# Mixer tiles of a two-layer model: one product of 512 columns for two of 256, in a ring of four PSUM banks

## The reference, cut to what matters

```python
def short_conv_mixer(h, w_in, conv_w, w_out):  # h: 256 tokens x 1024
    bg, cg, v = jnp.split(h @ w_in, 3, axis=-1)
    return (bg * causal_dwconv(cg * v, conv_w)) @ w_out

x = x + short_conv_mixer(rmsnorm(x, mix_norm[0]), a_w_in[0], a_conv[0], a_w_out[0])
x = x + conv_ffn(rmsnorm(x, ffn_norm[0]), ...)          # 2816 hidden features
...                                                      # attention layer, second conv_ffn, final norm
```

## Time and profile before

| | us |
|---|---|
| median of 3 runs | 623.72 (623.45 to 626.21) |
| the profiled execution | 623.19 |
| its span, from first to last instruction | 621.1 |
| TensorE busy | 606.9 (98%) |
| VectorE busy | 484.5 (78%) |
| ScalarE busy | 390.1 (63%) |
| mean granted TensorE clock | 0.999 |

### The profile page before, as it was taken

The page is one execution under the profiler, slowest core; times in us unless marked ns, Lnnn a source line. Parts: engine busy times, 40 slices in busy tenths (PEclk is TensorE's granted clock), DMA queues, the critical chain, the costliest instruction groups (busy, mean ns, idle before and its releaser), DMA issues.

```text
span 621.1 us, 11391 instructions
## 1 busy us (share of the span) xinstructions
PE 606.9 (98%) x3772; PEld 532.6 (86%) x3772; DVE 484.5 (78%) x954; ACT 390.1 (63%) x725; POOL 64.1 (10%) x82
## 2 busy tenths in 40 slices
PE   8999999999999999999999899999999999999995
PEld 8999998988888888888989777777988888888884
DVE  4888657788888887777877799938688888887765
ACT  7545336666666666668556488727766666666644
POOL 0110011000000000011131156610100000000010
PEclk9999999999999999999999999999999999999999
DMA  8797442465565655761476401033355555555521
GB/s 343 290 337 241 169 141 97 155 218 200 188 222 201 201 204 186 281 246 36 136 246 211 133 2 35 2 102 136 123 204 208 201 204 203 202 203 188 193 101 68
DMA packets 30352, 109.55 MB, mean 176 GB/s; under 512 B 3387, under 2 KB 3659, under 8 KB 30188
## 3 DMA queue, kind: packets, MB, share of 16 engines
q1 hardware_dynamic: 29756, 106.97, 48.9%
q0 software_dynamic: 560, 2.12, 1.0%
HBM read 108.01 MB, written 1.07 MB: 176 GB/s over the span
## 4 chain that ended last, share of the span: by engine, by line
PE 89%; DVE 5%; ACT 3%; issue 1%; DMA 1%; POOL 0%; DVEq 0%; ACTq 0%
PE bank L1244 24%; PE bank L1248 12%; PE bank L1193 10%; PE bank L1194 10%; PE bank L1195 10%; PE bank L1212 9%; PE bank L1217 4%; PE bank L1289 2%; DVE w_lo L814 1%; PE bank L1302 1%; PE bank L1571 1%; ACT work L557 1%; PE bank L1603 1%; PE bank L1596 1%; ACT w_hi L553 1%
## 5 line engine op out<-in xcount | busy, mean ns | idle before, releaser
L814 DVE TENSOR_TENSOR w_lo<-staged,w_hi 128x1024 fp32r<-128x1024 f32 x188 | 233.1, 1248 | 45.1 <-ACT w_hi L553 45.1
L553 ACT ACTIVATE w_hi<-staged 128x1024 fp32r<-128x1024 f32 x196 | 198.6, 1046 | 24.6 <-PE bank L1217 7.7
L1244 PE MATMUL bank<-gx,w_hi 128*128 128x512 f32 x640 | 159.4, 391 | 0.0
L1244 PEld LDWEIGHTS bank<-gx,w_hi 128*128 128x128 f32 x640 | 117.5, 188 | 23.0 <-DVE work L950 0.2
L1248 PEld LDWEIGHTS bank<-gx,w_lo 128*128 128x128 f32 x640 | 87.3, 190 | 6.3
L1248 PE MATMUL bank<-gx,w_lo 128*128 128x256 f32 x640 | 89.2, 282 | 0.0
L1193 PE MATMUL bank<-w_hi,y 128*128 128x512 f32 x208 | 81.5, 392 | 0.0
L1194 PE MATMUL bank<-w_lo,y 128*128 128x512 f32 x208 | 81.5, 392 | 0.0
L1195 PE MATMUL bank<-w_hi,y 128*128 128x512 f32 x208 | 80.9, 389 | 0.0
L683 ACT ACTIVATE work<-work,params 128x256 f32<-128x256 f32 x96 | 44.2, 504 | 54.3 <-DVE work L950 39.2
L697 ACT ACTIVATE y<-work 128x256 fp32r<-128x256 f32 x52 | 21.7, 418 | 77.6 <-DVE work L971 59.8
(11 more groups left out here) (182 smaller groups left out, 815.6 us busy)
## 6 DMA issues: line engine op xcount, KB each, us to landing
staged<-in_f_up SPq DMA_DIRECT2D x88, 512.0 KB, 5.1
staged<-in_f_down SPq DMA_DIRECT2D x44, 512.0 KB, 3.6
staged<-in_a_up SPq DMA_DIRECT2D x24, 512.0 KB, 6.9
staged<-in_b_up SPq DMA_DIRECT2D x24, 512.0 KB, 4.2
staged<-in_a_down SPq DMA_DIRECT2D x8, 512.0 KB, 3.6
staged<-in_b_down SPq DMA_DIRECT2D x8, 512.0 KB, 4.2
bias<-bias_rows POOLq DMA_DIRECT2D x1, 2048.0 KB, 12.1
x<-in_xt SPq DMA_DIRECT2D x1, 1024.0 KB, 9.2
```

Source lines behind the costliest of these rows:

```text
L553: nc.scalar.activation(w_hi[:, q["slot"], 0:n], staged[:, s, 0:n], ACT.Copy).then_inc(hi, 1)
L814: nc.vector.tensor_tensor(w_lo[:, q["slot"], 0:n], staged[:, s, 0:n], w_hi[:, q["slot"], 0:n].bitcast(F32), ALU.subtract).then_inc(lo, 1)
L1244: nc.tensor.matmul(dst, w_hi[:, s, kt * P:kt * P + P], gx[:, kt, :], start=kt == 0, stop=False, skip_group_check=True)
```

## The change

A mixer tile takes a whole bank. For each k-slice one product of 512 columns is made of w_hi and both parts of x, and one of 256 of w_lo and x_hi: 16 matmuls for 24. Tile (k, c) uses bank (3 (k % 2) + c) % 4, so over two units the banks go 0, 1, 2, 3, 0, 1 and start again. Before a tile whose bank was used before, TensorE waits for a count of `added`. For each tile ScalarE copies the bank's second half to the place of the result in SBUF (`parts_of`), VectorE adds the first half to it and counts `added`; the products with rstd, rstd2 and the third part follow on the sums in SBUF. The third sum stands behind the `early` remainder on VectorE, and the third copy behind the `early` lead on ScalarE. Line numbers in the changed kernel are higher: L553 becomes L563, L814 L835, L1212 and L1217 L1275 and L1279, L942 and L943 L968 and L970, L945 L976; new are L693 (the copy) and L964 (the sum).

```diff
--- before.py
+++ after.py
@@ -237,7 +237,8 @@
         squared, halved, deviated, rstd_done = sem("squared"), sem("halved"), sem("deviated"), sem("rstd_done")
         rstd_spread, rstd_ready, xn_done, xn_far, x_turned = (
             sem(n) for n in ("rstd_spread", "rstd_ready", "xn_done", "xn_far", "x_turned"))
-        lo_read = {s: sem(f"lo_read_{s}") for s in ("f0", "f1")}
+        lo_read = {s: sem(f"lo_read_{s}") for s in ("a", "f0", "f1")}
+        added = sem("added")
         padded = sem("padded")
         consts_done, table_done, rows_done, rows_copied = sem("consts_done"), sem("table_done"), sem("rows_done"), sem("rows_copied")
         rows_stored = sem("rows_stored")
@@ -317,6 +318,15 @@
         def split_of(st, t, kt):
 
             return SPLIT_AT[st] + 8 * t + kt + 1
+
+        def tile_bank(k, c):
+
+            return bank[(3 * (k % 2) + c) % 4]
+
+        def parts_of(k, c):
+
+            r = k % 2
+            return {0: shifted[:, r, 1, 2:2 + T], 1: conv[:, r, 1, :], 2: shifted[:, r, 0, 2:2 + T]}[c]
 
         def pair_of(st, k, n):
 
@@ -671,8 +681,19 @@
                 r = k % ring
                 u = k + PER[st] * i
                 early, middle, late = ahead
-                for q in early:
-                    lead(*q)
+                if st == "a":
+
+                    if k >= 2 or looped(i):
+                        act.wait_ge(y_lo_done["a"], u - 1)
+                    for c in range(3):
+                        if c == 2:
+                            for q in early:
+                                lead(*q)
+                        act.wait_ge(used_up, piece_of("a", "up", k, c)["n"] + 1 + stride("a", "up") * i)
+                        nc.scalar.activation(parts_of(k, c), tile_bank(k, c)[:, T:2 * T], ACT.Copy).then_inc(lo_read["a"], 1)
+                else:
+                    for q in early:
+                        lead(*q)
                 if st != "a":
 
                     act.wait_ge(used_up, piece_of(st, "up", k, 1)["n"] + 1 + stride(st, "up") * i)
@@ -936,14 +957,23 @@
                 u = k + PER[st] * i
                 early, middle, late = ahead
                 if st == "a":
-                    last = piece_of(st, "up", k, 2)
-
-                    dve.wait_ge(used_up, last["n"] + 1 + stride(st, "up") * i)
-                    nc.vector.tensor_tensor(shifted[:, r, 1, 2:2 + T], bank[2 * r][:, 0:T], rstd[:], ALU.mult)
-                    nc.vector.tensor_tensor(conv[:, r, 1, :], bank[2 * r][:, T:2 * T], rstd2, ALU.mult).then_inc(convolved[st], 1)
+
+                    def add(c):
+
+                        dve.wait_ge(lo_read["a"], 3 * u + c + 1)
+                        nc.vector.tensor_tensor(parts_of(k, c), tile_bank(k, c)[:, 0:T], parts_of(k, c), ALU.add).then_inc(added, 1)
+                        dve.wait_ge(added, 3 * u + c + 1)
+
+                    add(0)
+                    nc.vector.tensor_tensor(parts_of(k, 0), parts_of(k, 0), rstd[:], ALU.mult)
+                    add(1)
+                    nc.vector.tensor_tensor(parts_of(k, 1), parts_of(k, 1), rstd2, ALU.mult).then_inc(convolved[st], 1)
+                    for q in early:
+                        rest(*q)
+                    early = []
+                    add(2)
                     dve.wait_ge(convolved[st], 3 * u + 1)
-                    nc.vector.tensor_tensor(shifted[:, r, 0, 2:2 + T], bank[2 * r + 1][:, 0:T], conv[:, r, 1, :],
-                                            ALU.mult).then_inc(scaled[st], 1)
+                    nc.vector.tensor_tensor(parts_of(k, 2), parts_of(k, 2), parts_of(k, 1), ALU.mult).then_inc(scaled[st], 1)
                     halves, per, off = 1, 3, 1
                 else:
                     dve.wait_ge(lo_read[st], u + 1)
@@ -1225,13 +1255,30 @@
                 return nc.tensor.matmul(out_ap[:, 0:T], w_lo[:, s, cols], gx_hi[:, kt, :], start=False, stop=stop, skip_group_check=True)
 
             def up_a(k, i=0, cs=range(3)):
-                if k >= 2:
-
-                    pe.wait_ge(scaled["a"], k - 1 + PER["a"] * i)
+
                 for c in cs:
-                    fresh = (gx_lo_done, 0) if (k, c) == (0, 0) else (None, None)
-                    dst = bank[2 * (k % 2) + c // 2][:, c % 2 * T:(c % 2 + 1) * T]
-                    product(piece_of("a", "up", k, c), dst, gx_hi, gx_lo, c % 2 == 0, stride("a", "up") * i, *fresh)
+                    q, dst = piece_of("a", "up", k, c), tile_bank(k, c)
+                    s, move = q["slot"], stride("a", "up") * i
+                    if (k, c) != (1, 0) and k >= 1:
+
+                        last = {(0, 0): 2, (0, 1): 3, (1, 1): 1, (1, 2): 2}.get((k % 2, c), 0)
+                        pe.wait_ge(added, 3 * (k - 1 + PER["a"] * i) + last)
+                    if (k, c) == (0, 0):
+                        pe.wait_ge(lo_up, q["n"] + 1)
+                        for kt in range(KT):
+                            pe.wait_ge(gx_lo_done, kt + 1)
+                            mm = both(dst, s, kt, kt == 0, kt == KT - 1)
+                        mm.then_inc(used_up, 1)
+                        continue
+                    pe.wait_ge(hi_up, q["n"] + 1 + move)
+                    for kt in range(KT):
+                        nc.tensor.matmul(dst, w_hi[:, s, kt * P:kt * P + P], gx[:, kt, :], start=kt == 0, stop=False, skip_group_check=True)
+
+                    pe.wait_ge(lo_up, q["n"] + 1 + move)
+                    for kt in range(KT):
+                        mm = nc.tensor.matmul(dst[:, 0:T], w_lo[:, s, kt * P:kt * P + P], gx_hi[:, kt, :], start=False, stop=kt == KT - 1,
+                                              skip_group_check=True)
+                    mm.then_inc(used_up, 1)
 
             def up_f(st, k, i=0):
                 if k >= 2:
```

## The result

The changed kernel takes **634.38 us** (median of 4 runs, 633.43 to 636.28) against 623.88 of the kernel before: 1.0172 of it, 95% interval 1.0154 to 1.0190, 10.5 us slower. Forecast were 631.7 (628.9 to 633.8): the sign held, the range missed by 0.6 us. The profiled execution takes 634.81 us, 11.6 more than that of before.

The account below looks back on a forecast made before the run. TensorE was taken to bound the kernel. A saving of 2.5 us against stalls of 2.9 and 5.7 gave +6.1; with 1.9 for the clock, the forecast median was 631.7 us, range 628.9 to 633.8.

Parts of the forecast that it names:

- TensorE's own work: Mixer tiles: the change saves 0.11 us a tile, nothing on tile (0,0); over 23 tiles -2.5 us.
- What the halves cost: Mixer units: three copies add 1.4 us to ScalarE, three sums 1.3 to VectorE; free while neither is behind.
- VectorE's step when it is behind: Mixer, from unit 0's first sum to the next unit's: 10.4 us, bounds 9.8 and 11.0.
- First stall: Before tile (1,1), TensorE waits for the sum of (0,0) and starts at 22.45: +2.9 us.
- Second stall: Before tile (2,0), TensorE waits for the sum of (1,1) until 33.70: +5.7 us.
- The clock: In the second stall, idle 5.6 us, the granted clock falls to half; the restart costs 1.9 us, bounds 0 and 2.5.
- Behind it: Mixer after the second stall: no later bank wait shows, 0.4 us of slack stay at y_lo; all +6.1 us carried.
- a gap behind 40 us: Sign in the new trace that the prediction is wrong: TensorE gaps after 40 us, where it expected none.
- C: Rival: VectorE bounds the whole mixer stage if a step passes 11.06 us; +12.4 us, 636; chance 0.09.
- B: Rival: both stalls come but the clock doesn't fall; 629.8 us; chance 0.36.
- D: Rival: faster, the second bank wait is over before TensorE comes; at best 621.2 us; chance 0.04.
- E: Rival: no change, saving and stalls partly cancel; 623 to 625 us; chance 0.03.

Follow-up runs that it names:

- e9: The changed kernel with units 0 to 3 in the old form, down tiles 6 and 7 placed as in e3, steps written out: 622.87 us.
- e11: The kernel before, all eight units in the old form, with e9's places for down tiles 6 and 7 and its written-out steps: 623.63 us.
- e4: The changed kernel with products of ones into unused banks filling TensorE's three waits, to keep the clock up: 634.06 us.
- e1: The changed kernel with down tile 6's lead and remainder moved from the early to the middle slot of step 6: 632.59 us.
- e2: The changed kernel with down tile 7's remainder made by VectorE, late slot of step 6, instead of GpSimd: 635.29 us.
- e3: The changed kernel with down tile 6 in step 6's middle slot, down tile 7 in step 7's early slot, its remainder off GpSimd: 630.32 us.
- e5: The changed kernel with tiles (1,1) and (1,2) in empty banks 6 and 7, removing TensorE's first two bank waits: 635.77 us.
- e7: The changed kernel with units 0 and 1 in the old form and e3's places for down tiles 6 and 7: 629.34 us.
- e10: e3 with products of ones filling TensorE's first two waits, as in e4: 629.59 us.
- e8: The changed kernel with one more VectorE product of 256 columns in each mixer step, its result unused: 638.13 us.
- e6: The changed kernel with units 0 and 1 in the old form, units 2 to 7 in the new: 635.87 us.

## Why the prediction was wrong, and where it held

- **TensorE's own work**: right in kind. A tile saves 2.88 - 2.79 = 0.09 us, not 0.11; 23 of them 2.1, not 2.5. e9 shows that this saving reaches the end where nothing waits. Tile (0,0) costs more than before, which I had at nothing: tile (0,1) starts at 10.62 instead of 10.13.
- **What the halves cost**: VectorE's sum 0.42 (forecast 0.43), ScalarE's copy 0.38 (0.45). Right, though one of the copy's two bounds was misread: L967 of the earlier trace rows is VectorE's product with bg, not a copy.
- **VectorE's step when it is behind**: 10.38 against 10.4 in unit 0, within 0.02. In unit 1 it is 10.99, beside GpSimd's copies, and in the loop 10.68 to 10.73: neither was foreseen. Of the 0.3 us between the written-out steps (10.38, and e9's 10.40) and the looped ones most lies at the two taps: VectorE waits 0.79 to 0.82 us for ScalarE's tap, in e9 0.58, and its second tap starts 0.63 or 0.64 behind the first, in e9 0.52. The old form shows the second of these as well (0.62 in the loop, 0.51 written out in e11). That it is the loop's register instructions, on a chain that the new order leaves bare, is argued from this and wasn't tried by itself.
- **First stall**: its end was right; TensorE started at 22.29, forecast 22.45. The gap is 2.09 us and not 2.9, since the work ahead of it ended at 20.20 and not at 19.52. That the clock falls behind it wasn't forecast. It cost 1.66 us of TensorE's time and nothing of the kernel's (e4), since the second stall came after it and was only 3.80 us long instead of 5.7.
- **Second stall**: right; (2,0) at 33.47, forecast 33.70.
- **The clock**: the cost was near, 4.38 - 2.79 = 1.59 us in the second stall, forecast 1.9, but that it came was luck. The forecast rested on an idle time of 5.6 us against 5.05 at the end of the trace; the idle time was 3.80, and by that reasoning the clock should have stayed up. It fell after 2.09 us too.
- The last downs start at 98.93 against 91.24, +7.7; forecast were 6.1 + 1.9 = +8.0. Up to here the sum stood, with the clock's smaller cost making up for tiles that saved less.
- **Behind it, the step that failed.** "0.4 us of slack stay. So all of it is carried": the prediction had y_lo of unit 7 waiting for TensorE, since VectorE "gains 0.66 us a unit". It was the reverse: TensorE waited for y_lo, and the prediction's own sign of being wrong, a gap behind 40 us, is this one. With 10.4 a step, unit 7's first sum would have come at 94.8; it came at 99.91. The 5.1 us are 1.8 from the steps of units 1 to 5 (0.6 in unit 1, 1.2 in the four looped ones), with 0.15 off for the earlier start, and 3.5 from step 6, whose third copy stands behind a lead that waits for its weights (4.6 us later, less about 1 for one remainder fewer). The prediction had this wait at nothing without a reason: it put the third copy behind the early lead and never asked what that lead waits for, though the trace of before has its 5.01 us. Then 1.7 for the product that GpSimd holds. TensorE waited 3.17 us, and the clock fell for another 1.7: together 4.9, less 0.4 that before were a wait ahead of the transposes. With the +7.7 this is the 12.2 of the traces. e1, e2 and e3 show the two causes: with one of them taken away the third wait shrinks to 1.03 and 1.96 us, with both it is gone.
- By V the first two stalls are not what is paid in the change as it stands. e5 removes them and gains nothing, e4 removes their clock falls and y_lo comes no earlier. That they count where the end is mended fits e3, where TensorE waits for nothing behind them, but it is argued: e7 changes VectorE's queue too, and e10's gain isn't clear of the spread.
- **The rivals.** C named the mechanism, VectorE as the bound of the whole stage, and had chance 0.09, because I let it decide only where a step passes 11.06 us. No step but the seventh did. But a queue that is behind from the start, and gains only 11.12 - 10.7 = 0.4 us a unit on TensorE (3 x 2.79 + 2.75), is the bound without that; its condition was wrong, and I priced its waits as an average of steps where one wait for a transfer did most of it. B fell: the clock did fall. D and E fell with the first stall.

## What to carry to other kernels

Where a change puts an engine behind, follow that engine's queue to the end of the stage, step by step, with the DMA that each instruction waits for, before asking what the other engine's stalls cost; a saving of 2 us on the busiest engine is little against one wait of 4 us for a transfer in the queue of the engine that now leads. Such a wait can already stand in the trace of before, where it costs nothing, and the transfer can be late because the lagging engine frees its place late. Put what waits for it behind what the next engine waits for, and give the new form only to those units where there is room for its extra work (e9). To see which engine leads, lengthen or shorten one at a time: 8 us given to TensorE were worth nothing, 3.4 us of work added to VectorE cost 3.75.

## What the runs showed of the hardware that I had not expected

- A VectorE product of 256 columns with both inputs in SBUF took 2.09 us (e1: 2.00) beside GpSimd's subtraction, 0.42 without it (e2), and the sum that reads one input from PSUM took 0.42 beside it. The Trainium skill, "SBUF — State Buffer", section "SBUF: two separate sides", states that VectorE with two SBUF inputs and GpSimd share a pair of ports as an exclusive lock held for a whole instruction. The trace agrees: VectorE's product ended at 102.46, 0.28 us behind GpSimd's subtraction (99.70 + 2.48 = 102.18), and in e1 it was 0.28 as well.
- The clock fell after waits far shorter than the 5 us that I had from the end of the trace, but not each time: in the change after 2.09, 3.80 and 3.17 us, in e8 after 1.76, in e2 after 1.76 and 1.96, in e5 after 3.25; not in e1 after 1.69, in e3 after 1.84, nor in e6 and e7 after 3.3. It can fall when TensorE has already started again (in the change, with (1,1) started at 22.29, it is 1.00 from 22 to 23 us and 0.51 from 23 to 24), or while TensorE still waits (in e3 0.50 from 31 to 32, the tile behind starting at 32.65). Either way what a stall costs is partly paid behind it. The Trainium skill, "TensorE: Matmul & The Clock Gate", section "Why this matters for your kernels", warns against idle gaps between matmuls; the runs agree that gaps bring it on, and show that the length of one gap alone doesn't tell whether.
- In some executions the clock also fell in the attention layer (0.86 at 350 to 360 us in e2, 0.83 there in e5, and 0.84 at 330 to 340 in e9; e4, e6 and e10 have it too, the other profiled executions don't), with TensorE busy there and without a wait. Microsecond by microsecond it is the same fall to 0.50. 10 us at 0.86 and 0.84 are 1.4 and 1.6 us of TensorE's work; what brings it on stays open.
